# Two transformer blocks on one core: casts, row scalings and turns set in another order around the closings

## The reference, cut to what matters

```
mix = concatenated mixer outputs @ w_out
h = h + rms_norm(mix, ln_mix_post)      # closing of a part
a = rms_norm(h, ln_ffn_pre)             # input of the next part
ff = ... ; h = h + rms_norm(ff, ln_ffn_post)

rms_norm(x, g):  x * rsqrt(mean(x*x) + EPS) * g
headwise_rms_norm: the same over the 64 features of each head
```

## Time and profile before

| | us |
|---|---|
| median of three runs | 1534.03 |
| lowest and highest | 1532.83, 1535.18 |
| profiled execution, its own time | 1539.16 |
| its span | 1537.4 |
| PE busy | 1487.7 (97%) |
| DVE busy | 811.2 (53%) |
| ACT busy | 574.2 (37%) |
| POOL busy | 317.6 (21%) |

### The profile page before, as it was taken

One profiled execution on the slowest core, in us unless ns is written; L12 is line 12 of the kernel. 1 busy time (PEld: TensorE's weight loads), 2 busy tenths in 40 slices (PEclk: granted clock), 3 DMA queues, 4 the chain that ended last, 5 costly groups with the idle time before them and its releaser, 6 DMA issues. The chain is left out here.

```text
span 1537.4 us, 18663 instructions
## 1 busy us (share of the span) xinstructions
PE 1487.7 (97%) x7584; PEld 1213.5 (79%) x7584; DVE 811.2 (53%) x1122; ACT 574.2 (37%) x905; POOL 317.6 (21%) x304
## 2 busy tenths in 40 slices
PE   7999999999999999999998999998899999999998
PEld 5888788876788888888887776777778888888886
DVE  4232434588656536343347799778746344323425
ACT  4231544457626313233234421475325222112322
POOL 1000100000123896000003389534422000000000
PEclk9999999999999999999999999999799999999999
DMA  5232222220042232323242222110013323232322
GB/s 185 86 106 63 78 82 77 76 83 1 29 151 83 82 110 82 110 82 110 82 137 66 82 84 82 35 56 29 29 55 110 107 86 110 83 110 82 110 69 83
DMA packets 38858, 129.25 MB, mean 84 GB/s; under 512 B 4676, under 2 KB 23004, under 8 KB 27380
## 3 DMA queue, kind: packets, MB, share of 16 engines
q1 hardware_dynamic: 38484, 127.93, 24.4%
q10 hardware_dynamic: 288, 0.12, 0.0%
HBM read 124.82 MB, written 3.17 MB: 83 GB/s over the span
## 5 line engine op out<-in xcount | busy, mean ns | idle before, releaser
L266 PE MATMUL bank<-xT_hi,ring_hi 128*128 128x512 f32 (+2 forms) x928 | 355.3, 383 | 7.3 <-DVE xT_lo L1728 4.8
L266 PE MATMUL bank<-xT_hi,ring_lo 128*128 128x512 f32 (+2 forms) x928 | 352.1, 379 | 0.0
L266 PE MATMUL bank<-xT_lo,ring_hi 128*128 128x512 f32 (+2 forms) x928 | 352.1, 379 | 0.0
L247 DVE TENSOR_TENSOR ring_lo<-ring_raw,ring_hi 128x2048 fp32r<-128x2048 f32 (+3 forms) x112 | 260.1, 2324 | 170.3 <-ACT ring_hi L233 170.2
L233 ACT CAST ring_hi<-ring_raw 128x2048 fp32r<-128x2048 f32 (+4 forms) x114 | 210.9, 1852 | 242.2 <-DMA ring_raw<-in_w_ff 131.0
L266 PEld LDWEIGHTS bank<-xT_hi,ring_hi 128*128 128x128 f32 (+1 forms) x928 | 174.0, 188 | 48.3 <-issue 8.1
L266 PEld LDWEIGHTS bank<-xT_hi,ring_lo 128*128 128x128 f32 (+1 forms) x928 | 174.1, 188 | 33.7
L266 PEld LDWEIGHTS bank<-xT_lo,ring_hi 128*128 128x128 f32 (+1 forms) x928 | 174.1, 188 | 32.5
L266 PE MATMUL bank<-ring_hi,hid_hi 128*128 128x512 f32 x416 | 162.1, 390 | 0.0
L266 PE MATMUL bank<-ring_hi,hid_lo 128*128 128x512 f32 x416 | 161.9, 389 | 0.0
L266 PE MATMUL bank<-ring_lo,hid_hi 128*128 128x512 f32 x416 | 161.9, 389 | 0.0
(11 more groups left out here) (503 smaller groups left out, 2169.8 us busy)
## 6 DMA issues: line engine op xcount, KB each, us to landing
ring_raw<-in_w_ff SPq DMA_DIRECT2D x30, 1024.0 KB, 4.8
ring_raw<-in_w_up SPq DMA_DIRECT2D x22, 1024.0 KB, 4.9
ring_raw<-in_w_proj SPq DMA_DIRECT2D x8, 1024.0 KB, 5.2
ring_raw<-in_w_gates SPq DMA_DIRECT2D x8, 1024.0 KB, 4.9
ring_raw<-in_w_fm SPq DMA_DIRECT2D x12, 512.0 KB, 4.7
ring_raw<-in_w_dn_a SPq DMA_DIRECT2D x6, 1024.0 KB, 4.8
ring_raw<-in_w_proj SPq DMA_DIRECT2D x8, 512.0 KB, 4.6
ring_raw<-in_w_out SPq DMA_DIRECT2D x4, 1024.0 KB, 4.8
```

What stands on the lines that cost most here:

```text
L247: k.nc.vector.tensor_tensor(k.ring.lo[:, g % SLOTS, 0:n], k.raw[:, g % SLOTS, 0:n], plain(k.ring.hi[:, g % SLOTS, 0:n]), ALU.subtract).the ...
L266: mm = k.nc.tensor.matmul(out, x, y, start=first and n == 0, stop=last and n == 3 * len(pairs) - 1)
```

## The change

It has three pieces.

- In the closings' ACT queue, `split_hi` of the chunk `self.end` moves from tile 1 to tile 0, ahead of `square_h(0)`, and `normalise(t - 1)` moves ahead of `square_y(t, 1)`.
- In the closings' DVE queue, `split_lo` of that chunk moves from tile 1 to tile 0, behind the mean of h's squares.
- In the mixers' end, fox's turns move into the stage before it, `stat` and mlstm's turns move between products, and the second chunk's products wait for each bank apart. DVE reads mlstm's banks ahead of hgrn2's.

```diff
@@ Closing.pe
                     for t in range(T):
+                        if t == 2:
+                            self.lead.stat(pe, free)
                         product(p, t, c, True, False, slice(0, 2))
-                    self.lead.stat(pe, free)
                     self.lead.fox_ready(pe)
                     for t in range(T):
+                        if t == 2:
+                            self.lead.turn_ml(pe, free)
                         mm = product(p, t, c, False, False, slice(2, 4))
                     mm.then_inc(k.w_used.sem, 1)
                     self.lead.spread_out(pe, free)
                     continue
-                if self.lead is not None:
-                    self.lead.banks_free(pe)
...
                 for t in range(T):
+                    if self.lead is not None:
+                        self.lead.bank_free(pe, t)
@@ Closing.act
         for t in range(T):
+            if norm and t:
+                self.normalise(act, t - 1)
             self.square_y(act, t, 1)
-            if t == 1:
+            if t == 0:
                 split_hi(k, act, self.end + 1)
             if norm:
-                if t:
-                    self.normalise(act, t - 1)
                 self.square_h(act, t)
@@ Closing.dve
-            if t == 1:
-                split_lo(k, dve, self.end + 1)
             if norm:
                 dve.wait_ge(self.sq_h.sem, self.sq_h.base + 2 * t + 2)
                 mean(8 + 2 * t, T + t)
+            if t == 0:
+                split_lo(k, dve, self.end + 1)
+            if norm:
                 if t == T - 1:
@@ stage_recurrent, PE, behind its last step
+
+            pe.wait_ge(sel.sem, sel.base + 4 * nl)
+            pe.wait_ge(end.fox_scaled.sem, end.fox_scaled.base + 1)
+            end.turn_fox(pe, (k.pb[1], k.pb[3]))
@@ MixerEnd
+    def turn_ml(self, pe, free):
+
+        k = self.k
+        pe.wait_ge(self.mean.sem, self.mean.base + 1)
         pe.wait_ge(self.ml_scaled.sem, self.ml_scaled.base + 1)
...
-    def banks_free(self, pe):
-
-        pe.wait_ge(self.ml_lo.sem, self.ml_lo.base + 2)
-        pe.wait_ge(self.scaled.sem, self.scaled.base + 2)
+    def bank_free(self, pe, t):
+
+        s = self.ml_lo if t < 2 else self.scaled
+        pe.wait_ge(s.sem, s.base + t % 2 + 1)
@@ MixerEnd.dve
+        for f in range(2):
+            dve.wait_ge(self.ml_hi.sem, self.ml_hi.base + f + 1)
+            v.scalar_tensor_tensor(out=self.mlT.lo[:, f, :], in0=free[f][:, :], scalar=col(k, "mix_gain2", 6 + f),
+                                   in1=plain(self.mlT.hi[:, f, :]), op0=ALU.mult, op1=ALU.subtract).then_inc(self.ml_lo.sem, 1)
         for p in range(2):
             dve.wait_ge(self.spread.sem, self.spread.base + p + 1)
...
-        for f in range(2):
-            dve.wait_ge(self.ml_hi.sem, self.ml_hi.base + f + 1)
```

More of the change, by code:

```diff
@@ L3506, in close_stage, with turn_fox @@
             s.base += 1
-    def begin(self, pe, free):
+    def turn_fox(self, pe, free):
         k = self.k
@@ L3514, in begin @@
             mm.then_inc(self.fox_turned.sem, 1)
+    def begin(self, pe, free):
+        k = self.k
         at = {(0, 1): (0, 0), (2, 3): (0, 1), (0, 2): (1, 0), (0, 3): (1, 1), (1, 2): (1, 2), (1, 3): (1, 3)}
@@ L3616, in dve @@
                                    op1=ALU.mult).then_inc(self.scaled.sem, 1)
-        for f in range(2):
-            dve.wait_ge(self.ml_hi.sem, self.ml_hi.base + f + 1)
-            v.scalar_tensor_tensor(out=self.mlT.lo[:, f, :], in0=free[f][:, :], scalar=col(k, "mix_gain2", 6 + f),
-                                   in1=plain(self.mlT.hi[:, f, :]), op0=ALU.mult, op1=ALU.subtract).then_inc(self.ml_lo.sem, 1)
         for p in range(2):
```

## The result

The changed kernel takes 1539.52 us (median of 15 runs, 1538.27 to 1543.49), the kernel before in the same session 1533.97 (15 runs, 1532.04 to 1539.36). The ratio is 1.0028, with a 95% interval of 1.0018 to 1.0038: slower by 4.3 us. The two medians lie 5.6 apart and the two means 5.0, since this ratio is not that of the medians. The forecast was 1538.9, slower. Two runs of the experiments, one of the kernel before at 6405.53 us and one of the closings alone at 2487.53, had granted clocks of 0.22 and 0.56 and are left out of every comparison.

The account below looks back on a forecast made before the run. PE, busy 97% of the span, was taken as the bound. Closings +9.3, mixers' end -6.2 and closings' clock +1.7 gave 4.8 us slower: 1538.9 from a median of 1534.03, range 1532 to 1543.

Parts of the forecast that it names:

- Cast, split, root: mix1's closing: cast costs nothing, the split delays POOL's root by 2.05 us, scaling starts at 468.15, 0.3 later than before.
- The one row at 550.99: Trace row of before: POOL's operation behind a waiting split took 3.09 us, against 1.04 alone; basis for the split's order.
- Rival 1: Closings: POOL's root slips in ahead of the split, closings cost only 4.3, total 1532.1 us; chance 12%.
- The ring: Closings: scaling, squares, mean, add, product, root pace tiles 1 to 3 at 7.15 us (mlp1 7.5); closings +9.3 us.
- Rival 2: Closings: the ring doesn't close, PE paces the tiles and waits for scaled rows go; 1522.5 us; chance 8%.
- The mixers' end: Fox's turns moved and the bank wait removed win 6.2 us, with bounds 4.6 and 7.7.
- 2.5 for the turns: Mixers' end: moving fox's turns off the stage's start wins 2.5 us, the middle between a returning and a never-falling clock.
- 1.7 for the second fall: Mixers' end: the clock's second fall, behind the bank wait, costs 0.34 x 5 = 1.7 us and goes with that wait.
- If it never falls, 0.44 x 7 = 3.1 more is won: Mixers' end, stage's boundary: without the first clock fall, 3.1 us more than the turns' 0.9 is won.
- Clock in the closings: Last wait becomes 1.9 us in three closings; one clock fall of three at 1.7 us, bounds none and two.
- Rival 3: Mixers' end wins only 2.9 instead of 6.2: clock falls as before or turns wait; 1542.1 us; 15% together with rival 4.
- Rival 4: Longer waits bring the low clock into all three closings, 5.1 instead of 1.7 us; 1542.3; 15% together with rival 3.

Follow-up runs that it names:

- closings alone: Kernel before plus only the reordering in the closings' ACT and DVE queues, mixers' end as before: 1544.28 us, ratio 1.0058.
- split held back: Changed kernel, with DVE's split at tile 0 also waiting for POOL's root of tile 0's h: 1537.55 us, ratio 1.0008.
- before again: The kernel before, unchanged, run once more for a second profile: one run of 1537.08 us, span 1535.3.
- mixers' end only: Kernel before plus only the change's mixers' end, closings as before: ratio 0.9964; in a second session 1530.34 us, ratio 0.9963.
- fox's turns only: Kernel before plus only the move of fox's turns ahead of the stage's boundary: 1532.13 us, ratio 0.9992.
- the scaling back and the split held: Changed kernel, scaling back behind the squares, split waiting for tile 0's root; run twice: 1531.03 us, ratio 0.9974, then 1528.59, ratio 0.9951.
- the scaling alone moved: Changed kernel with cast and split back at tile 1, so only the scaling is moved in the closings: 1543.51 us, ratio 1.0045.

## Why the prediction was right, and where it was not

**Cast, split, root.** Right to 0.2 us each: cast at 460.54 (460.6), split at 463.85 for 3.64 (463.95, 3.7), root 2.61 (2.6), scaling at 468.00 (468.15). The one row at 550.99 was the right guide. Rival 1, the root slipping in ahead, did not occur in any closing (2.61, 2.60 and 2.60); it could be made, with the split held back, and gave 3.1 us. By the rule cited from the Trainium skill ("SBUF — State Buffer", "Who interferes with whom") the trace agrees with the exclusive holding, and it adds the order: a waiting split of 2048 columns goes in between two POOL operations queued back to back.

**The ring.** Right: 7.1 per tile against 7.15 in mix1, and in mlp1 the adds from tile 1 on stand 7.5 apart against 7.5. Rival 2 fell. PE resumes 3.37, 2.20 and 3.32 us later, 8.9 in all; I had 3.45, 2.4, 3.45, or 9.3. All pieces of the ring came from rows of before. The last wait, 1.9 in my sum, reads 1.74 in mlp1 and 1.73 in mix2.

**The mixers' end.** The moves of work came out as worked out, the clock did not, and with it the size. From PE's last `v_one` products to the first product of the third chunk (its rows; the last is `hgT_hi`):

| kernel | from | to | us |
|---|---|---|---|
| before, profiled | 1098.99 | 1143.13 | 44.14 |
| before again | 1101.34 | 1141.04 | 39.70 |
| closings only | 1102.48 | 1142.15 | 39.67 |
| changed | 1102.65 | 1139.31 | 36.66 |
| mixers' end only | 1096.33 | 1133.03 | 36.70 |
| fox's turns only | 1098.80 | 1139.08 | 40.28 |

At full clock the change is worth 39.70 - 36.66 = **3.0**, of which 1.0 is fox's turns (from the last `v_one` products to the first of hgrn2's values 1106.36 - 1101.34 = 5.02 in before again, 1106.68 - 1102.65 = 4.03 now). The other 2.0 is the wait for banks and PE's restart, as I had worked out. Fox's turns only stands at 40.28 and not near 38.7 because its trace has the second fall, which costs 1.6 there. The rest of my 6.2, that is 1.5 of the 2.5 for the turns and the whole 1.7 for the second fall, was two clock falls that only some executions have. The failed step is "If it never falls, 0.44 x 7 = 3.1 more is won", and the 1.7 behind it: I took one profiled execution's clock for the kernel's. In the profiled pair the mixers' end shows 7.5; alone, in timings, 5.5.

**Why 5.5 and not 3.0.** Most runs of the kernel before fall into two groups, and every run has its granted clock with it. Of 72 runs in the sessions of the experiments, 32 lie at 1531.4 to 1534.5 us (mean 1533.1, clock 0.9918), 34 at 1536.6 to 1539.4 (mean 1538.4, clock 0.9886), and six between. The clock's difference, 0.0032 x 1535 = 4.9 us, is nearly the whole 5.3 between them. But it does not hold run by run: 27 of the 34 have a clock of 0.987 to 0.989, and seven, at 1537.6 to 1538.0, have 0.991, as many of the short ones do. What makes these seven long is not shown, and no trace of them exists.

The 19 runs of the mixers' end alone show no second group: 1528.9 to 1534.2, mean 1530.8. That is 2.3 below before's short group, near the 3.0 of the traces, and 7.6 below the long one; mixed half and half, 5. The changed kernel has no clear second group either: 12 runs from 1538.6 to 1542.4, mean 1540.2, clock 0.9909, and in the session of the result 15 from 1538.3 to 1543.5, mean 1539.7. The 12 are 7.1 above before's short group and 1.8 above the long one. Less 1.4 for the clock, an estimate from (0.9918 - 0.9909) x 1535, the 7.1 is 5.7, where the traces give 8.9 - 3.0 = 5.9. So the change loses 6 us of work order, and about half of before's runs are 5 us long by themselves, most of them with a low clock.

What makes an execution of before join the long group stays open: the one other execution of it with a trace (1537.08) has its low clock elsewhere, and no execution of the short group was profiled. Nor is the low clock bound to the old mixers' end: four of eleven runs with the scaling back and the split held have 0.988 or 0.989, and all six with the scaling alone moved have 0.985 to 0.989. Fox's turns alone put 8 of 11 runs at 1531.2 to 1533.2, so moving them may be what thins the long group; 11 runs don't settle it.

**Clock in the closings.** I took one fall of three at 1.7. In the profiled execution of the change there was none, in the second one there were two, both in mlp1: behind the wait for the first turn, and where PE resumes. PE's first turns and the stretch of the resumption, the changed kernel first and then its second execution:

```profile
830.56 1.09 PE L1505 MATMUL bank<-ident,cl_xn_mlp 128*128 128x128 f32 x8 [2.36 <-ACT cl_xn_mlp L1619]
...
854.00:859.00 5.00, 4.82 (x40) 4.82 (x41) 0.99 (x2) 0.00 (x0) 0.00 (x0) 1.00 0.00 0
```

```profile
831.60 1.97 PE L1505 MATMUL bank<-ident,cl_xn_mlp 128*128 128x128 f32 x8 [2.36 <-ACT cl_xn_mlp L1619]
...
854.00:859.00 5.00, 3.77 (x19) 3.78 (x20) 2.04 (x3) 0.84 (x2) 0.00 (x0) 0.66 0.00 0
```

The waits are the same in both, 2.36 ahead of the turn and 1.74 ahead of the resumption; the eight turns take 1.09 at full clock and 1.97 at half. The first fall cost nothing in the end, for the ring sets the pace there: from mlp1's first mean to the resumption it is 32.63 in the second execution and 32.62 in the first. The second fall comes behind the resumption and does cost: DVE's next split starts 8.7 us behind the resumption in the first execution (862.92) and 10.2 behind it in the second (865.44), 1.5 later. (The whole span is 1.9 longer, but 1.1 of that was there before the resumption.) So the term is a matter of the execution: 0 in one, 1.5 in the other, against my 1.7.

**The sum.** 9.3 - 6.2 + 1.7 gave 4.8; measured 4.3 by the ratio, 5.0 by the means, 5.6 by the medians. By the parts it should read 8.9 - 3.0 = 5.9, plus about 1.4 for the change's own clock, less what before's runs lie above their short group. In the session of the result this is 1.6 (four of 15 at 1536.7 or more, mean 1534.7 against 1533.1), so 5.7; in the sessions of the experiments about 2.6, so 4.7. My total came near by luck: the mixers' end was taken 3.2 too high, because I took one execution's clock for the kernel's, and 1.7 for the closings' clock and the longer runs among before's happened to cover most of it. Rival 3's price for the mixers' end, 2.9, was the better one for the order of work, though its reason (the clock falls as before) did not hold: the clock behind both places is 1.00 in the change. Rival 4 did not occur as put: no fall in one execution of the change, and in the other two, of which one counted.

## What to carry to other kernels

Before you move an operation ahead of another in one queue, ask whether its own input depends on what it is put in front of, through other engines: if so you close a ring, and its length, summed from rows, has to be set against the pace of the engine that bounds the kernel. A scaling that is wanted early by PE is not worth putting ahead of squares that feed the next root. And a clock fall seen behind an idle time in one execution is not yet a cost in every execution: compare the granted clocks of all runs first, and look whether they make groups. Where a ring sets the pace, slow products can cost nothing; where PE sets it, the same fall shows in full.

## What the runs showed of the hardware

- A DVE split of 2048 columns that waits while POOL works is served between two POOL operations queued in a row: the 128x1 root behind it took 2.61 us instead of 0.56, once in each of three closings. Here are POOL's roots grouped, the changed kernel and then the one with the split held back (count, busy us, mean ns, idle before):

```profile
L1656 POOL TENSOR_TENSOR stat<-stat 128x1 f32<-128x1 f32 x28 | 24.0, 858 | 651.5 <-DVE stat L1697 651.5
```

```profile
L1656 POOL TENSOR_TENSOR stat<-stat 128x1 f32<-128x1 f32 x28 | 18.3, 652 | 655.6 <-DVE stat L1697 655.6
```

- A semaphore wait that holds the split back until POOL's pair of operations is done shortened the split from 3.64 to 2.29 us and the root from 2.61 to 0.56. Started 2.0 us later, it ended 0.7 us later.
- The granted clock fell to half behind idle times of 1.58 and 1.83 us in one execution of a program, and stayed at full speed behind idle times of 1.59 and 1.83 in another execution of the same program. Behind a wait of 3.80 us eight turns took 1.09 us in one execution and 1.97 in another, and the closing mlp1 was 2.6 us longer for it; in the changed kernel, behind a wait of 2.36, the same slow turns (1.09 and 1.97) left it at 32.6 both times.
- Two groups of run times 5.3 us apart, in one program on one core, go with mean granted clocks of 0.9918 and 0.9886, a difference worth 4.9 us; seven of the 34 long runs have 0.991 all the same.
